# Units 22 and 23 of each mixing layer join the three existing pairs of gate units as seven block products

## The reference

```
z = h @ w_in                      # its last 4 * 1024 columns are the gate logits
for m in the four mixers:
    merged += sigmoid(gate_logits[m]) * (mixer_out[m] @ w_branch[m])
x = x + rms_norm(merged @ w_mix_out, ln_mix_post)
```

## Time and profile before

| | |
|---|---|
| median of 3 runs | 2704.27 us (2704.24 to 2704.9) |
| the profiled execution's own time | 2704.16 us |
| its span, first to last instruction | 2702.4 us |
| PE busy | 2647.8 us, 98% of the span |
| DVE, ACT, POOL busy | 1331.8, 425.9 and 109.2 us |
| PE clock granted | 0.999 of full speed |
| mixing layer 0, end of unit 20 to start of L1341's second product | 278.06 to 326.20 us |
| mixing layer 1, the same stretch | begins 667.74 us later |

### The profile page before, as it was taken

The page is one execution under the profiler, slowest core; times in us unless marked ns, Lnnn a source line. Parts: engine busy times, 40 slices in busy tenths (PEclk is TensorE's granted clock), DMA queues, the critical chain, the costliest instruction groups (busy, mean ns, idle before and its releaser), DMA issues.

```text
span 2702.4 us, 47623 instructions
## 1 busy us (share of the span) xinstructions
PE 2647.8 (98%) x20746; PEld 2031.1 (75%) x20746; DVE 1331.8 (49%) x2386; ACT 425.9 (16%) x854; POOL 109.2 (4%) x134
## 2 busy tenths in 40 slices
PE   9999999999999999999999999999999999999997
PEld 6789997776688989777686887856777666666664
DVE  3654675776365467577654665546772111111112
ACT  2220222101222122200133111320110000000000
POOL 0011400000001130000000000000000000000000
PEclk9999999999999999999999999999999999999999
DMA  6322443544233143344433443339999999999996
GB/s 274 119 108 78 180 142 117 195 172 164 104 146 121 58 189 133 140 161 183 164 125 133 164 187 126 125 124 423 422 395 414 422 417 417 423 419 417 421 422 249
DMA packets 66999, 620.99 MB, mean 230 GB/s; under 512 B 7584, under 2 KB 7968, under 8 KB 11488
## 3 DMA queue, kind: packets, MB, share of 16 engines
q1 hardware_dynamic: 63072, 602.26, 55.8%
q0 software_dynamic: 2720, 13.52, 1.3%
q10 hardware_dynamic: 992, 2.10, 0.2%
HBM read 614.70 MB, written 3.15 MB: 229 GB/s over the span
## 4 chain that ended last, share of the span: by engine, by line
PE 85%; DMA 7%; DVE 6%; ACT 1%; issue 1%; SPq 0%; DVEq 0%; ACTq 0%
PE ps L1445 11%; PE ps L857 9%; PE ps L1457 8%; PE ps L1879 7%; PE ps L1277 6%; PE ps L899 5%; PE ps L1869 4%; DMA fbT<-in_od_exp_w 4%; PE ps L1946 3%; PE ps L1839 2%; PE ps L1866 2%; PE ps L1908 2%; PE ps L836 2%; PE ps L1341 2%; PE ps L1289 2%; PE ps L1255 2%
## 5 line engine op out<-in xcount | busy, mean ns | idle before, releaser
L1869 PE MATMUL ps<-slabA,work 128*32 128x128 f32 x2016 | 228.0, 273 | 0.0
L1866 PE MATMUL ps<-slabA,work 128*32 128x384 f32 x2016 | 225.2, 488 | 0.0
L1879 PE MATMUL ps<-fbT,work 128*64 128x256 f32 x1792 | 209.0, 383 | 9.1 <-DMA fbT<-in_od_exp_w 9.1
L1869 PEld LDWEIGHTS ps<-slabA,work 128*32 128x32 f32 x2016 | 216.7, 110 | 0.0
L3633 DVE COPY work<-ps 128x192 f32<-128x192 f32 x42 | 15.0, 358 | 400.0 <-PE ps L836 400.0
L1277 PE MATMUL ps<-hT,slabA 128*128 128x256 f32 x832 | 188.9, 380 | 1.1 <-ACT work L2214 1.1
L1879 PEld LDWEIGHTS ps<-fbT,work 128*64 128x64 f32 x1792 | 122.0, 137 | 79.1 <-DMA fbT<-in_od_exp_w 18.1
L1277 PEld LDWEIGHTS ps<-hT,slabA 128*128 128x128 f32 x832 | 155.7, 190 | 23.4 <-ACT work L2214 1.9
L857 PE MATMUL ps<-hT,slabA 128*128 128x256 f32 x736 | 163.4, 381 | 0.0
L1445 PEld LDWEIGHTS ps<-work 128*128 128x128 f32 x1152 | 139.5, 192 | 21.5 <-issue 21.0
L857 PEld LDWEIGHTS ps<-hT,slabA 128*128 128x128 f32 x736 | 138.3, 190 | 20.5 <-issue 2.5
(11 more groups left out here) (555 smaller groups left out, 4256.5 us busy)
## 6 DMA issues: line engine op xcount, KB each, us to landing
fbT<-in_od_exp_w SPq DMA_DIRECT2D x168, 1024.0 KB, 11.9
slabA<-in_od_exp_w SPq DMA_DIRECT2D x56, 2048.0 KB, 15.7
slabB<-in_od_exp_w SPq DMA_DIRECT2D x56, 1024.0 KB, 15.8
slabA<-in_w_in SPq DMA_DIRECT2D x24, 2048.0 KB, 8.3
slabA<-in_mlp_w SPq DMA_DIRECT2D x16, 2048.0 KB, 9.4
slabB<-in_mlp_w SPq DMA_DIRECT2D x32, 1024.0 KB, 4.8
slabA<-in_ev_ffn_w SPq DMA_DIRECT2D x11, 2048.0 KB, 8.1
slabA<-in_xa_wkv SPq DMA_DIRECT2D x6, 2048.0 KB, 8.1
```

Of the source, the lines that this page charges most:

```text
L1866: mm(rows[QUAD * i:QUAD * (i + 1)], tokens, wk[:, :, 0:2 * MID], start=(k == 0), stop=(k == KD - 1), skip_group_check=True)
L1869: last = mm(rows[MID:P, :, 64 * i:64 * (i + 1)], tokens, wk[:, :, 2 * MID:T], start=(k == 0 and i == 0), stop=(k == KD - 1), skip_group_ch ...
L1879: last = mm(ps[SMALL * j:SMALL * (j + 1), 1, 0:2 * P].rearrange("p (w n) -> p w n", w=2), xs[:, KD // 2 * h + k, :], v[:, k, :, j * P:(j + ...
```

## The change

`gate_pairs` becomes (22, 24, 26, 28). All places that used the first entry follow: the transposes move to stand behind unit 20 and ahead of unit 21, units 22 and 23 go through `gate_pair`, and the banks of units 30 and 31 are renumbered. Slab (2, 1), with units 20 to 23, is now given back by the pair's two PSUM groups and not by unit 23.

```
-        gate_pairs = (24, 26, 28)
+        gate_pairs = (22, 24, 26, 28)
...
         def side_bank(u):
-            return u % PROJ
+            return (u if u <= gate_pairs[-1] else u - 4 * KD + 2 + gate_pairs[0]) % PROJ
...
-                        ringA.load(sp, [cols(w, IN_SLABS, GATE0 + m * D + half * 512)], groups(4) if (i, half) == (3, 0) else None)
+                        ringA.load(sp, [cols(w, IN_SLABS, GATE0 + m * D + half * 512)], groups({(2, 1): 2, (3, 0): 4}[i, half]) if (i, half) in ((2, 1), (3, 0)) else None)
...
-                    n = first_gates + gate_pairs[i] // 4 - gate_pairs[0] // 4
+                    n = first_gates + gate_pairs[i] // 4 - (gate_pairs[0] + 3) // 4
```

## The result

| | before | changed |
|---|---|---|
| median of 19 runs | 2703.78 us | 2708.74 us |
| all runs | 2702.59 to 2706.62 | 2706.32 to 2711.04 |
| ratio to before | | 1.0018, 95% interval 1.0012 to 1.0024 |
| profiled execution: time, span | 2704.16, 2702.4 us | 2707.45, 2705.6 us |

The changed kernel is 5.0 us slower, within the 5.4 us that the prediction called no change. The forecast was 2708.1 us, 3.86 over the kernel before. The changed kernel's runs are spread over 4.7 us.

A forecast was written before the change was run, and what follows sets the result against it. PE, busy 98% of the span, was taken to bound the kernel. Per layer 0.56 + 2.02 - 0.65 gave 1.93 us, 3.86 for two: 2708.0, on the median 2708.1; range for 8 in 10: 2705.6 to 2709.9.

The forecast's parts named there:

- Pair against two units, 0.65 a layer: Units 22 and 23 on PE: a pair takes 7.98 us against 8.64 for two plain units, a gain of 0.65 a layer.
- The wait at the transposes: Behind unit 20, PE waits for L3105's rows: 0.46 plus 0.10 for restarting, a loss of 0.56 us a layer.
- only one of the waits counts: Rival: one wait counts, or DVE's sums have the port alone and the second wait shrinks to 1.25; 2706.6 us, chance 0.10.
- the second wait: PE's wait inside pair 22 for DVE's four sums: 1.92 us plus 0.10 for restarting, 2.02 a layer.
- The pair sums, 3.62: DVE's four sums for pair 22 take 3.62 us as in the trace, from 283.41, ready at 287.03; bounds 2.85 to 4.49.
- the rows' mix: Of pair 22's four sums on DVE, two take 1.1 us beside POOL and two 0.69, again 3.62.
- The restart, 0.10: On PE, a group of matmuls that had to wait takes 0.10 us more, 1.10 against 1.00.
- PE's waits are too short to cost clock: The granted clock on PE stays at 1.00, as in the stretch with its wait ahead of 326.20; no time added.
- Everything behind pair 22 on time: Only the first pair's sums are late; pairs 24 to 28 and the tail move as a whole, 1.93 us later.
- Slower beyond what can be told (0.06): Rival: POOL's operations come between all four sums, which take over 4.4 us; 2709.7 us or more, chance 0.06.

The follow-up runs named there:

- the delayed kernel: The kernel before with four unread subtractions on DVE ahead of pair 24's sums: 2709.17 us, then 2709.68; with nine unread PE matmuls filling the wait 2706.82.

## Why the prediction was right, and where it was not

The mechanism was right: PE waits for the pair sums, since DVE's chain to them has lost its head start. The increase was forecast at 3.86 us and measured at 5.0. The time itself, 2708.1 against 2708.74, came closer than that, and this was luck: the kernel before, on whose 2704.27 it was built, has a median of 2703.78 over 19 runs.

- **Pair against two units, 0.65 a layer:** right, and shown by itself by the kernel with early sums and later transposes (13.03 against 13.68).
- **The wait at the transposes:** its size was right (0.45 for 0.46), its place in the sum was not. The prediction listed 0.56 as a term and took "only one of the waits counts" for a rival. It is a piece of the same wait: what PE does not wait at the transposes it waits at the sums, 2.72 in place of 1.88. The sum came out right because the second wait had been counted from PE's late arrival, so that the 0.56 cancels. Where this wait does stand alone, with the early sums, it costs 0.67 and not 0.56.
- **The pair sums, 3.62:** measured 283.59 to 287.27 = 3.68, two of 0.69 and two of 1.10. The rule of the Trainium skill ("SBUF — State Buffer", "Who interferes with whom"), that the shared port is an exclusive lock, had given 0.07 more than the rows' mix; here the trace agrees with it. POOL's L794, begun at 285.67, ends at 286.72, and DVE's L2717, begun at 286.17, ends 0.54 later.
- **The restart, 0.10:** too small. The 20 matmuls behind the wait take 4.73 in the chain against 4.46 without one (40/56 of 6.25), 0.27. With the 0.06 of the sums this makes the +2.17 of layer 0, where 1.93 was predicted. The 0.27 does not come with the length of the wait: with the wait filled, PE idles 0.1 us and the 20 matmuls still take 4.73.
- **"PE's waits are too short to cost clock":** wrong, and the one claim that failed outright. It rested on a stretch with a wait of 0.45 us; the new one is 1.9. In both profiles of the changed kernel the clock fell to half behind it in layer 1, for 6.36 - 4.73 = 1.6 us, and with the wait filled the median is 1.25 lower. Of the 1.1 us between 3.86 and 5.0, the restart and the sums explain 0.5 (0.24 a layer); the remaining 0.6 is put down to the clock, which would be 1.6 if it fell once in every execution. How often it falls was not measured. The profiles show only that it does not fall at each wait: same wait, layer 0, clock 1.00.
- **Everything behind pair 22 on time:** right. PE has no wait at pairs 24 to 28 (4.73 and 1.73, then 6.25 and 1.73 without a gap), and the tail moved as a whole, 12.44 us in both.
- **Slower beyond what can be told (0.06):** POOL came between two of the four sums and not all. What took the time from +3.9 to +5.0, 0.4 short of that line, was the restart and, by the argument above, the clock, neither of which the rival had in it.

## What to carry to other kernels

A block product with fewer multiplications moves work from PE to whoever makes the sums, and filler ahead of it is also that engine's head start: before turning two filler units into such a product, subtract them from the slack of the sums, and add back only the idle time that this engine has ahead of them (here 1.7 us of slack, 8.6 us of filler gone, 4.57 us of idle time on DVE). Waits of one engine in a row on one chain are one wait: price the last, and expect nothing from removing an earlier one alone. Where a wait on TensorE grows from half a us to two, allow for the clock as well. Look for an idle stretch further up into which the sums fit: here that took the whole loss away.

## What the runs showed of the hardware

- Behind a wait of 1.9 us, with waits of 0.45 some 8 us before, TensorE's granted clock fell from 2.4 to 1.2 GHz (1.00 to 0.50) at about 958 us and was back before 963, in two of four such places in the profiles of the changed kernel, both in layer 1; behind waits of 2.1 and 2.7 us it stayed at 1.00 in all six profiled places. Keeping PE busy with unread matmuls for the same time took 1.25 and 2.9 us off the medians.
- The clock also fell to 0.50 behind waits for a load near the end of the program: behind 1.29 us in the filled version of the delayed kernel and behind 2.12 us in the kernel with early sums, while one of 1.36 us, at 2613.67 in the kernel with later transposes, left it at 1.00. The first of the two, which is only a little shorter than the one that left the clock alone:

```profile
2578.00:2580.00 2.00, 1.07 (x6) 0.69 (x8) 0.78 (x3) 0.00 (x0) 0.00 (x0) 0.79 1.04 426
2580.00:2582.00 2.00, 2.00 (x12) 1.18 (x10) 0.00 (x0) 0.00 (x0) 0.00 (x0) 0.50 0.97 410
```

- The Trainium skill ("TensorE: Matmul & The Clock Gate", "HAM oscillation — how this bites in real kernels") warns of idle gaps that send the clock down. The traces agree with the direction; that the same gap did it in layer 1 and not in layer 0 is what these runs add.
- A DVE operation of 128x512 with both inputs in on-chip memory takes 0.69 us alone and 1.03 to 1.18 when one of POOL's began first and still ran; with POOL's cut to one column, all of it came back.
